# Full-depth multiplies, two maps in one bank and a moved lead-in in a two-architecture transformer kernel

## The reference, cut to what matters

```python
s = jnp.einsum('bhmqd,bhmkd->bhmqk', q_blk, k).astype(jnp.float32) * scale
p = jax.nn.softmax(jnp.where(mask, s, -jnp.inf), axis=-1)
a = p[:, :, 0] - lam * p[:, :, 1]
return jnp.einsum('bhqk,bhkd->bhqd', a.astype(v.dtype), v)
```

```python
s = jnp.einsum('bkgqd,bksd->bkgqs', qblk, kh)
p = jax.nn.softmax(s, axis=-1)
return jnp.einsum('bkgqs,bksd->bkgqd', p.astype(vh.dtype), vh)
```

## Time and profile before

| | |
|---|---|
| Time, median of 3 runs | 4322.69 us (4320.81 to 4325.49) |
| The profiled execution's own time | 4329.32 us |
| Its span | 4327.5 us |
| PE busy | 3994.0 us, 92% of the span |
| DVE, ACT, POOL busy | 2089.6, 1235.4, 456.6 us |
| Granted TensorE clock, mean | 0.933 of full speed |
| Chain that ended last | PE 86%, DVE 6%, issue, POOL 2% each |
| Largest group | L1919, weight strips, 68% of that chain |

### The profile page before, as it was taken

How to read it: one execution, slowest core, us unless ns; L and a number is a source line. 1 busy time by engine, 2 the same in 40 slices (tenths; PEclk the granted TensorE clock), 3 DMA queues, 4 the chain that set the end, 5 groups by cost and what they waited for, 6 DMA issues and landing times.

```text
span 4327.5 us, 66111 instructions
## 1 busy us (share of the span) xinstructions
PE 3994.0 (92%) x25446; PEld 3545.8 (82%) x25446; DVE 2089.6 (48%) x2552; ACT 1235.4 (29%) x1691; POOL 456.6 (11%) x478
## 2 busy tenths in 40 slices
PE   7997999799799979998998999999999998999997
PEld 4665877466587869997997889998998897889997
DVE  5557763554776354424445454324433434544433
ACT  2433332233233222213123322212222312332221
POOL 1123110212311020000002000000000000200001
PEclk9988999898899979998998899998999998899998
DMA  3111223111122312232110222222222111022222
GB/s 106 35 44 63 93 87 102 67 35 43 61 95 87 102 64 91 83 100 68 55 59 1 67 75 87 87 98 81 87 88 95 64 50 49 11 78 75 90 88 87
DMA packets 124513, 313.64 MB, mean 72 GB/s; under 512 B 48385, under 2 KB 48385, under 8 KB 124129
## 3 DMA queue, kind: packets, MB, share of 16 engines
q1 hardware_dynamic: 122944, 302.25, 21.3%
q0 software_dynamic: 1440, 9.61, 0.6%
HBM read 309.57 MB, written 2.10 MB: 72 GB/s over the span
## 4 chain that ended last, share of the span: by engine, by line
PE 86%; DVE 6%; issue 2%; POOL 2%; DMA 1%; ACT 1%; SPq 1%; DVEq 0%; POOLq 0%; ACTq 0%
PE acc L1919 68%; PE acc L1978 5%; DVE x_lo L993 2%; PE misc L2552 1%; DVE sumsq L987 1%; PE misc L1919 1%; PE acc L2523 1%; SPq L378 1%; PE acc L2534 1%; PE misc L2397 1%; PE acc L2539 1%; PE misc L2102 1%; PE acc L1961 1%; PE misc L1955 1%; PE misc L2020 1%
## 5 line engine op out<-in xcount | busy, mean ns | idle before, releaser
L1919 PE MATMUL acc<-x_hi,w_hi 128*128 128x264 f32 (+1 forms) x4880 | 1198.8, 314 | 204.4 <-DVE x_lo L993 169.7
L432 ACT CAST w_hi<-stage 128x1024 fp32r<-128x1024 f32 x568 | 595.6, 1049 | 2161.2 <-PE acc L1919 1962.0
L1919 PE MATMUL acc<-x_lo,w_hi 128*128 128x264 f32 (+1 forms) x4880 | 1179.1, 310 | 0.0
L1919 PE MATMUL acc<-x_hi,w_lo 128*128 128x264 f32 (+1 forms) x4880 | 1175.7, 309 | 0.0
L1919 PEld LDWEIGHTS acc<-x_hi,w_hi 128*128 128x128 f32 x4880 | 806.6, 193 | 293.4 <-issue 135.1
L965 DVE TENSOR_TENSOR w_lo<-stage,w_hi 128x1024 fp32r<-128x1024 f32 x568 | 762.1, 1342 | 568.7 <-ACT w_hi L432 558.3
L1919 PEld LDWEIGHTS acc<-x_hi,w_lo 128*128 128x128 f32 x4880 | 807.8, 194 | 37.0
L1919 PEld LDWEIGHTS acc<-x_lo,w_hi 128*128 128x128 f32 x4880 | 808.7, 194 | 35.3 <-issue 1.0
L1919 PE MATMUL acc<-ff_hi,w_hi 128*128 128x264 f32 (+1 forms) x1760 | 429.0, 309 | 32.7 <-POOL ff_lo L1828 16.5
L1919 PE MATMUL acc<-ff_hi,w_lo 128*128 128x264 f32 (+1 forms) x1760 | 427.9, 308 | 0.0
L1919 PE MATMUL acc<-ff_lo,w_hi 128*128 128x264 f32 (+1 forms) x1760 | 426.7, 308 | 0.0
(11 more groups left out here) (310 smaller groups left out, 4100.3 us busy)
## 6 DMA issues: line engine op xcount, KB each, us to landing
stage<-weights SPq DMA_DIRECT2D x568, 512.0 KB, 3.3
rotary_decay<-tables POOLq DMA_DIRECT2D x2, 2048.0 KB, 8.5
consts<-consts POOLq DMA_DIRECT2D x4, 704.0 KB, 4.5
x<-x_in SPq DMA_DIRECT2D x1, 2048.0 KB, 8.3
lse_rows<-lse_columns SPq DMA_DIRECT2D x128, 0.5 KB, 2.0
max_rows<-max_columns SPq DMA_DIRECT2D x128, 0.5 KB, 2.0
out<-x SPq DMA_DIRECT2D x1, 2048.0 KB, 7.1
rotary_masks<-tables POOLq DMA_DIRECT2D x2, 784.0 KB, 4.8
```

The lines of the kernel that those rows point to most:

```text
L432: nc.scalar.copy(whi[p][:, :], stage[p][:, :]).then_inc(hi_ready, 1)
L1919: ins = mm(ps[:, b, 0:tn], ww, act_[:, kt, t0:t0 + tn], start=start and n == 0 and q == 0, stop=stop and n == last and q == 2)
```

## The change

- `KL1` holds the low part of k twice, over all 128 partitions, as `KK1` does; `k_lo` writes it with four VectorE instructions per head where there were two. `ON1`, `NM1`, `ON` and `NM` are cleared over all 128 partitions, with the ones in two rows. With that, the multiplies of S, T and N are 128 rows deep. Only the 16-token tile's values stay at 16 rows.
- The two maps are accumulated one after the other in the same bank. After the first four steps `half_out` copies the bank, the second map's first multiply starts it anew and waits for that copy, and `head_out` adds lambda times the bank to the copy. The factor lambda goes from `probs_hi` and `probs_lo`.
- `ret_pairs` issues two values and then two scores.
- The first 8 `scores` of attention2 are issued in mixer2 between its last nine strips, into `M[:, 2:4, :]` (`s2_slot`), and their maxima are taken there, the columns of the first head too. For that `k_hi`, `k_lo`, `q_hi` and `q_lo` come one to three strips earlier, and GpSimd prepares `ON` and `MX2` earlier. SyncE's queue is the same: the first head's row DMAs come after the last strip of mixer2 in it.

```diff
-            KL1 = sb("k1_lo", [P, 2, SEQ], F32R, c)
+            KL1 = sb("k1_lo_twice", [P, 2, 2, SEQ], F32R, c)
...
+        def s2_slot(s):
+
+            return acc[0] if s >= AHEAD else M[:, 2:4, :]
...
             def max_rows(h):
+                sp.wait_ge(ones2_ready, at(2, 2))
...
             def lse_rows(h, m):
                 b = h % 2
+                sp.wait_ge(causal_ready, at(2, 2))
...
                 g_inverse(2)
+                act.wait_ge(q_rope, at(5, 1))
+                k_hi(0)
+                k_hi(1)
                 split_hi()
                 g_inverse(3)
+                q_hi(0)
...
-                        ins = nc.vector.tensor_tensor(KL1[r, b, :], raw[r, :], KK1[r, b, m, :].bitcast(F32), ALU.subtract)
+                        for half in (slice(0, 64), slice(64, P)):
+                            ins = nc.vector.tensor_tensor(KL1[half, b, m, :], raw[r, :], KK1[r, b, m, :].bitcast(F32), ALU.subtract)
...
-                    if u < 4:
-                        ins = nc.vector.tensor_tensor(dst, src, hi_part, ALU.subtract)
-                    else:
-                        ins = nc.vector.scalar_tensor_tensor(dst, src, lam[:, 4:5], hi_part, ALU.mult, ALU.subtract)
-                    ins.then_inc(p1l_ready, 1)
+                    nc.vector.tensor_tensor(PL1[:, n % 3, 0:W], PF1[:, n % 2, 0:W], PH1[:, n % 3, 0:W].bitcast(F32),
+                                            ALU.subtract).then_inc(p1l_ready, 1)
+
+                def half_out(h):
+                    dve.wait_ge(pv1_done, at(32, 8 * h + 4))
+                    nc.vector.tensor_copy(PV[:, h, :], M[:, 2, :]).then_inc(o1_half, 1)
 
                 def head_out(h):
                     dve.wait_ge(pv1_done, at(32, 8 * h + 8))
-                    nc.vector.tensor_copy(PV[:, h, :], M[:, 2, :]).then_inc(o1_out, 1)
+                    dve.wait_ge(o1_half, at(4, h + 1))
+                    nc.vector.scalar_tensor_tensor(PV[:, h, :], M[:, 2, :], lam[:, 4:5], PV[:, h, :],
+                                                   ALU.mult, ALU.add).then_inc(o1_out, 1)
...
+                dve.wait_ge(ones2_ready, at(2, 1))
+                maxima(0)
                 split_lo()
                 g_gate(0)
                 g_gate(1)
                 strip_out(GT[:, 9, :])
+                maxima(1)
                 split_lo()
...
                 strip_out(GT[:, 12, :])
+                maxima(4)
+                max_columns(0)
...
                 strip_out(GT[:, 15, :])
+                maxima(7)
                 split_lo()
                 for h in range(4):
                     g_lo(h)
...
-                    if u < 4:
-                        ins = nc.gpsimd.tensor_copy(PH1[:, n % 3, 0:W], PF1[:, n % 2, 0:W])
-                    else:
-                        ins = nc.gpsimd.tensor_scalar(PH1[:, n % 3, 0:W], PF1[:, n % 2, 0:W], lam[:, 4:5], None, ALU.mult)
-                    ins.then_inc(p1h_ready, 1)
+                    nc.gpsimd.tensor_copy(PH1[:, n % 3, 0:W], PF1[:, n % 2, 0:W]).then_inc(p1h_ready, 1)
...
+                nc.gpsimd.memset(NM1[:, :, :].bitcast(F32), 0.0)
+                link(nc.gpsimd.memset(ON1[:, :].bitcast(F32), 0.0), pool_step, steps)
...
-                    mm(ps[:, 0:W], QS1[r, b, m, q], KL1[r, b, 0:W], start=False, stop=False)
+                    mm(ps[:, 0:W], QS1[:, b, m, q], KL1[:, b, m, 0:W], start=False, stop=False)
...
-                    mm(ps[:, 0:W], KL1[r, b, k], QS1[r, b, m, q], start=False, stop=False)
+                    mm(ps[:, 0:W], KL1[:, b, m, k], QS1[:, b, m, q], start=False, stop=False)
                     mm(ps[:, 0:P], CM1[:, 0, :], CM1[:, 2, :], start=False, stop=False)
-                    mm(ps[:, 0:W], ON1[0:2, :], NM1[0:2, m, q], start=False, stop=True).then_inc(t1_full, 1)
+                    mm(ps[:, 0:W], ON1[:, :], NM1[:, m, q], start=False, stop=True).then_inc(t1_full, 1)
...
+                    if u == 4:
+                        pe.wait_ge(o1_half, at(4, h + 1))
...
-                    for k in range(2):
-                        ret_values(j + k)
-                        if more:
-                            ret_scores(j + k + 2)
+                    ret_values(j)
+                    ret_values(j + 1)
+                    if more:
+                        ret_scores(j + 2)
+                        ret_scores(j + 3)
...
-                for _ in range(6):
+                strip_of()
+                strip_of()
+                pe.wait_ge(kl_ready, at(2, 2))
+                pe.wait_ge(att_ready, at(12, 12))
+                scores(0)
+                for n in range(1, 5):
                     strip_of()
+                    scores(n)
...
-                for _ in range(3):
+                for n in range(5, 8):
                     strip_of()
+                    scores(n)
                 all_evacuated()
...
-                        ins = mm(acc[1][0:nk, a, 0:HALF], ON[0:2, 0:nk], NM[0:2, h % 2, HALF * a:HALF * a + HALF],
+                        ins = mm(acc[1][0:nk, a, 0:HALF], ON[:, 0:nk], NM[:, h % 2, HALF * a:HALF * a + HALF],
                                  start=False, stop=True)
...
-                for n in range(-AHEAD, STEPS2 + 2):
+                for n in range(STEPS2 + 2):
```

More of the change, by code:

```diff
@@ L1198, in mixer1 @@
                 two(maxima, 1, 0)
+                half_out(0)
                 two(probs_lo, 0, 4)
@@ L1220, in mixer1 @@
                 two(maxima, 2, 0)
+                half_out(1)
                 two(probs_lo, 1, 4)
@@ L1243, in mixer1 @@
                 two(maxima, 3, 0)
+                half_out(2)
                 two(probs_lo, 2, 4)
@@ L1262, in mixer1 @@
                 strip_out(PR[:, 5, :])
+                half_out(3)
                 two(probs_lo, 3, 4)
@@ L1580, in mixer2 @@
                 split_lo()
+                k_lo(0)
+                k_lo(1)
                 strip_out(GT[:, 6, :])
@@ L1595, in mixer2 @@
                 strip_out(GT[:, 10, :])
+                maxima(2)
                 split_lo()
-                k_lo(0)
-                k_lo(1)
+                q_lo(1)
                 strip_out(GT[:, 11, :])
-                split_lo()
-                q_lo(0)
-                q_lo(1)
-                strip_out(GT[:, 12, :])
+                maxima(3)
                 split_lo()
                 q_lo(2)
+                strip_out(GT[:, 12, :])
+                maxima(4)
+                max_columns(0)
+                split_lo()
                 q_lo(3)
                 strip_out(GT[:, 13, :])
+                maxima(5)
                 split_lo()
                 strip_out(GT[:, 14, :])
+                maxima(6)
                 split_lo()
@@ L1655, in out @@
                                             ALU.mult).then_inc(on2_ready, 1)
-                dve.wait_ge(ones2_ready, at(1, 1))
-                for n in range(-AHEAD, STEPS2 + 4):
+                for n in range(STEPS2 + 4):
                     if n + AHEAD < STEPS2:
@@ L2100, in values @@
                             pe.wait_ge(ro_out, at(2, 2))
+                    if u == 4:
+                        pe.wait_ge(o1_half, at(4, h + 1))
                     for x, (v, p) in enumerate(((VH1, PH1), (VL1, PH1), (VH1, PL1))):
-                        ins = mm(o, v[:, b, j, :], p[:, n % 3, 0:W], start=u == 0 and x == 0, stop=u == 7 and x == 2)
+                        ins = mm(o, v[:, b, j, :], p[:, n % 3, 0:W], start=u in (0, 4) and x == 0, stop=u in (3, 7) and x == 2)
                     ins.then_inc(pv1_done, 1)
@@ L2294, in col, with scores @@
                 return (0, c0) if c0 < 272 else (1, c0 - 272)
+            def scores(s):
+                h, t = s // 5, s % 5
+                c0, nq = TILES2[t]
+                if t == 0 and h % 2 == 0:
+                    pe.wait_ge(qs_ready, at(4, h // 2 + 1))
+                if s:
+                    pe.wait_ge(s2_max, at(STEPS2, s))
+                for x, kk in enumerate((KK, KL)):
+                    for a in range(2):
+                        ins = mm(s2_slot(s)[0:nq, a, 0:HALF], QS[:, h, c0:c0 + nq], kk[:, h // 4, HALF * a:HALF * a + HALF],
+                                 start=x == 0, stop=x == 1)
+                ins.then_inc(s2_full, 1)
             def mixer2():
@@ L2512, in attention2 @@
                 pe.wait_ge(g_ln, at(4, 4))
-                def scores(s):
-                    h, t = s // 5, s % 5
-                    c0, nq = TILES2[t]
-                    if t == 0 and h % 2 == 0:
-                        pe.wait_ge(qs_ready, at(4, h // 2 + 1))
-                    if s:
-                        pe.wait_ge(s2_max, at(STEPS2, s))
-                    for x, kk in enumerate((KK, KL)):
-                        for a in range(2):
-                            ins = mm(acc[0][0:nq, a, 0:HALF], QS[:, h, c0:c0 + nq], kk[:, h // 4, HALF * a:HALF * a + HALF],
-                                     start=x == 0, stop=x == 1)
-                    ins.then_inc(s2_full, 1)
                 def scores_t(n):
```

71 lines of the change are left out of this document (36 added, 35 removed).

## The result

The changed kernel takes 4181.62 us (median of 4 runs, 4179.14 to 4186.91) where the kernel before takes 4324.09 on the same chip; the ratio is 0.9671, 95% interval 0.9654 to 0.9688. The forecast was 4198, range 4160 to 4242. The profiled execution took 4182.48 us; its span is 4180.7, 146.8 less than that of the profiled execution before. The medians differ by 142.5, since the profiled execution of before (4329.32) was slower than each of the four timed ones.

A forecast was written before the change was run, and what follows sets the result against it. TensorE was taken to set the pace in the changed stretches. Mixer1's 75.6 us and attention2's 48.5, together 124, took the profiled 4329.3 to 4205, or 4198 against the runs' median; range 4160 to 4242.

The forecast's parts named there:

- the rival of more clock: Mixer1 and attention2's opening: all 14 us per layer go to 2.4 GHz, giving 4180; chance 0.17.
- Depth in mixer1: Mixer1's attention: S, T and first value multiplies without depth changes save 61.6 us over eight heads.
- strip halves: Mixer1: a strip half that follows T saves about 0.1 us each, 4 us in all.
- Clock in mixer1: Mixer1's attention proper: half of 14 us per layer at 1.2 GHz goes, gaining 6 us in all (0 to 14).
- Lambda: Tail of mixer1's last head: GpSimd's rounding without lambda shortens the chain to V, 4 us in all.
- Costs in mixer1: Mixer1: extra VectorE work ahead of V costs 1.5 us, the fourth head's late row DMAs 2 us.
- the forecast's sign of being wrong: Mixer1: V waiting for probs_lo in the middle of heads would show the forecast wrong; no size given.
- Lead-in: Attention2's start: scores moved between mixer2's last strips let S(9) start 16 us earlier per layer, 32 in all.
- the cold start: Attention2's first loop steps may run at 1.2 GHz: a loss of 0 to 8 us per layer, 5 taken.
- Loop: Attention2's loop: 10.6 us per head, set by the row DMA chain; gains 13 and 10.5 us in the two layers.
- Tail: Attention2's end, the steps without S: gains 1.5 us per layer, 3 in all.
- The rival on the other side: Changed stretches of mixer1 and attention2: fully deep multiplies lower the granted clock, 4377 at share 0.35; chance 0.05.

The follow-up runs named there:

- e11: Changed kernel with KL1 multiplies back at 64 rows, subtraction's multiplies at 2 rows and lambda back in the rounding, one accumulation; ratio 0.9901 against the kernel before.
- e9: Changed kernel with both depth edits undone: KL1 multiplies at 64 rows, subtraction's multiplies at 2 rows; ratio 0.9916 against the kernel before.
- e1: Changed kernel with only mixer1's multiplies by KL1 back at 64 rows; ratio 0.9773 against the kernel before.
- e2: Changed kernel with only the multiplies that subtract the logarithm or the maxima back at 2 rows; ratio 0.9765 against the kernel before.
- e4: Changed kernel with lambda back in the rounding: both maps in one accumulation, no half_out; ratio 0.9706 against the kernel before.
- e3: Changed kernel with only attention2's lead-in back, the first 8 scores and their maxima taken there again; ratio 0.9751 against the kernel before.
- e8: Changed kernel with attention2's scores issued 9 steps ahead instead of 8; ratio 0.9645 against the kernel before.
- e6: Changed kernel with the subtraction's multiplies 66 rows deep instead of 128; ratio 0.9673 against the kernel before.
- e7: Changed kernel with the subtraction's multiplies 34 rows deep instead of 128; ratio 0.9750 against the kernel before.
- e10: e8 with two VectorE orders changed in mixer1 (v_lo ahead of split_lo, lse ahead of maxima and head_out); 4167.29 us, ratio 0.9638 against the kernel before.

## Why the prediction held, and where its terms were off

Undoing in order splits the gain of the profiled executions. In mixer1, from before to e11 (pairs, order) 8.4 us, e11 to e9 (lambda at the old pace, or the clock alone) 5.7, e9 to changed (depth) 71.0: 85.1. In attention2, before to e11 (the lead-in) 40.2, then 21.0 for depth: 61.2. The time came out 16 us below the forecast, in the range, at the rival of more clock (4180). The mechanism held: the longer intervals at changes of depth, the lead-in and the DMA chain that comes next were each shown by undoing or removing them. That the sum came so near owes something to luck, since mixer1's own time was put too high by some 5 us and the clock's share of the gain too low in every stage.

- *Depth in mixer1*: the prices read as differences of rows held. Forecast 65.6 with the strip halves, a head 8.2 us shorter. Measured: a head 8.3 us shorter (lambda and the order of retention in it), 0.16 and 0.12 us per change in e1 and e2. Without the clock the depth is worth 56 (e1 and e2) to 59 us (e9). Deep 128-column multiplies came at 0.05 to 0.12 against the 0.12 taken. All of mixer1's terms but the clock add up to 69.6 in the forecast and, up to the last value multiply, to 64.3 measured (82.8 less 18.5 of clock).
- *Clock in mixer1*: taken as 6 us (0 to 14); this was too small. The forecast put 14 of the 31 us at 1.2 GHz of a layer in the attention proper and let half of them go. The trace of before has 23.1 us in each layer up to the last value multiply, and all of it went: 46.2 us, 18.5 at the 0.4 us that a cold one cost, 23.1 at most. Undoing shows that it goes with depth, and mostly with both edits of it: the stage has 54.6 and 68.2 us cold in the two kernels with both undone, 20.4 and 30.7 with one. It is the largest of mixer1's mis-sized terms, and the forecast's reason for it, gaps in TensorE's work, can at most mean the longer intervals: 13.7 us per layer came with no wait.
- *Lambda*: the term "matters only in the tail of the last head, 4 in all" was priced with the slack of before, where V came microseconds after its data. That slack was TensorE's slowness, which the other edit removes. In the new kernel lambda would cost 13.5 (e4), in the old 5.7 at most (e11), and perhaps nothing. The forecast's sum is not much off for it, since depth with lambda left in would have gained that much less; the failure is in adding two terms that share a slack.
- *Costs in mixer1*: the waits stand where they were put: rows of the fourth head 1.04 and 1.28 us (2 forecast), `v_lo` behind `k_lo` 0.93 in each layer and V behind it 0.54 (1.5 forecast, 2.9 measured). The 0.54 is the forecast's sign of being wrong, V waiting for `probs_lo` in the middle of a head; it came once per layer and small. VectorE rose to 69% (67).
- *Lead-in*: S(9) came 16.7 us earlier per layer, 33.4 (32 forecast). The step that failed in size is the cold start, "0 to 8 us per layer, 5 taken" against the gain: the loop's cold stretches, from the first T to N(35), were 3.4 and 10.2 us, and those of before, 19.3 and 15.2, had been larger. Measured, the lead-in is worth 38 to 40 us (e3, e11) instead of 22. TensorE's 4 us of waiting ahead of S(9) did not bring what its 21 us had.
- *Loop*: the chain S, maximum, columns, ten DMAs, N became the pace, 10.6 us where no issue was slow and up to 11.6 where one was, as worked out; e8 shows it by removing it. From S(9) to N(35) the gain was 10.3 and 5.5 us, 15.8, against 13 + 10.5 - 10 = 13.5 with the cold start in it.
- *Tail*: 3 forecast, 11.2 measured (N(35) to the next strip 20.3 and 21.6 us before, 16.0 and 14.7 after). Its cold part fell from 14.9 and 17.7 us to 4.3 and 2.5, so most of this too is clock: two tails of e9 and e11 that had only 2.8 us of it took 16.5 and 16.4 us, so that the depth itself is worth some 1.8 per tail (1.5 forecast). In the five kernels with ones of 2 or 34 rows, 8 of 10 tails had 10 to 18 us at 1.2 GHz; in the eight with 66 or 128 rows, none of 16 had over 6.
- *The rival on the other side*, that fully deep work lowers the clock, did not come: the clock is 0.96 and 0.95 where before had 0.92 and 0.81.

Open: why the cold time of mixer1 comes back mostly when both depth edits are undone. Waits of TensorE are not what brings it in the attention proper, since before it waited for nothing from 92 to 262 us and had 13.7 us at 1.2 GHz there, while the changed kernel waits three times in that part of its work (1.0, 0.9 and 0.5 us) and has none. The kernels with fewer long intervals have less of it, but in single layers it scatters (the second layer of e2 has 20.5 us cold in mixer1, the first 10.2), and no run here separates the intervals from the depth itself.

## What to carry to other kernels

Read the price of a change of depth as the difference of start-to-start intervals of TensorE, not from the durations: here 0.12 to 0.16 us per change between 128 rows and 64, 34, 16 or 2, so pad short contractions with zero rows (up to 66 does as well as up to 128) where other deep multiplies stand around them. When TensorE gets faster, price every side chain again at the new pace, since slack of the old trace is not there any more, and look for the chain that is next (here ten small DMAs per head, hidden by issuing scores one step earlier). Where the stretch that gets denser has time at 1.2 GHz, find how much with windows over that stretch alone, and take part of it into the gain: here it was some 18 of 85 us in mixer1 and most of 11 in attention2's tail.

## What the hardware showed that was not expected

- A multiply 66 rows deep costs nothing against 128, one 34 rows deep costs as much as 2 rows (e6, e7): 0.24 us for the pair ahead of it with 66 rows, 0.34 with 2; 0.44 for the 34-row pair itself. Between 34 and 16 rows a change costs too (0.43 to 0.44), between 2 and 16 it does not (0.35).
- The granted clock rose as long intervals and waits went: over both attention2 stretches 109.2 us at 1.2 GHz before, 30.8 after the change, 13.6 with the row chain hidden as well (20.4 in e10). It had fallen without any wait, too: 13.7 us per layer in mixer1 before, with TensorE's list of waits empty.
- Some of the small row DMAs take 1.1 to 1.6 us from one issue to the next instead of 0.64 (6 of 144 intervals in the changed kernel), and a head of attention2 with such a one takes up to 1 us longer as soon as its chain sets the pace.
